# Query panels of a retrieval layer as three products of rounded operands, with the remainders taken by GpSimd

## What is computed

```
q = (xb @ w_q).reshape(PEER_BLOCK, PEER_HEADS, PEER_QDIM)       # 8 heads, 256 wide
s1 = jnp.einsum('phd,nd->phn', q[..., :half], subkeys[0])       # 128 keys
s2 = jnp.einsum('phd,nd->phn', q[..., half:], subkeys[1])
v1, i1 = lax.top_k(s1, PEER_TOPK)                               # 16 best of each half
v2, i2 = lax.top_k(s2, PEER_TOPK)
cand = (v1[..., :, None] + v2[..., None, :])                    # 256 candidates a head
cs, ci = lax.top_k(cand, PEER_TOPK)
...
g = jax.nn.softmax(cs); a = gelu(xb . u[e])                     # e: 16 of 16384 experts a head
y = sum over the chosen experts of g * a * v[e]
```

## Time and profile before

| what | value |
|---|---|
| three executions | 2624.45, 2632.71, 2630.9 us, median 2630.9 us |
| profiled execution, its own time | 2625.58 us |
| its span, first to last instruction | 2623.8 us |
| mean granted PE clock | 0.981 of full speed |
| busy: PE, PEld, DVE, ACT, POOL | 97%, 86%, 67%, 46%, 0% |
| query stage of layer 0 (first matmul to end of panel 7) | 735.67 to 798.21 us |
| query stage of layer 1 | 1753.61 to 1817.51 us |

### The profile page before, as it was taken

How to read it: one execution, slowest core, us unless ns; L and a number is a source line. 1 busy time by engine, 2 the same in 40 slices (tenths; PEclk the granted TensorE clock), 3 DMA queues, 4 the chain that set the end, 5 groups by cost and what they waited for, 6 DMA issues and landing times.

```text
span 2623.8 us, 42459 instructions
## 1 busy us (share of the span) xinstructions
PE 2543.8 (97%) x15716; PEld 2265.7 (86%) x15716; DVE 1765.4 (67%) x3521; ACT 1213.9 (46%) x2399; POOL 3.5 (0%) x10
## 2 busy tenths in 40 slices
PE   8999999999999999999999998989999999999997
PEld 4587889988889999999888887679999999888886
DVE  3662668865359977786788874537986787555554
ACT  2321124442214567775444443332457776455554
POOL 0000000000000000000000000000000000000000
PEclk9999999999999999999999999799999999999998
DMA  6562567656334544434777763123554443555553
GB/s 261 192 241 81 199 231 276 241 195 247 106 113 148 183 170 145 145 132 166 268 277 271 281 218 141 62 81 113 177 192 147 145 145 133 189 192 193 193 192 111
DMA packets 65348, 471.65 MB, mean 180 GB/s; under 512 B 7296, under 2 KB 7552, under 8 KB 8240
## 3 DMA queue, kind: packets, MB, share of 16 engines
q1 hardware_dynamic: 64656, 467.85, 50.1%
q10 hardware_dynamic: 272, 1.05, 0.1%
q0 software_dynamic: 272, 0.69, 0.1%
HBM read 468.51 MB, written 1.05 MB: 179 GB/s over the span
## 4 chain that ended last, share of the span: by engine, by line
PE 93%; DVE 5%; ACT 1%; issue 1%; DMA 1%; SPq 0%; DVEq 0%; ACTq 0%
PE bank L641 27%; PE bank L682 27%; PE bank L503 10%; PE bank L839 5%; PE bank L653 4%; PE bank L748 4%; PE bank L870 2%; PE bank L513 2%; PE bank L976 2%; PE bank L487 1%; PE bank L449 1%; PE bank L933 1%; DVE macc L1566 1%; PE bank L519 1%; PE bank L746 1%
## 5 line engine op out<-in xcount | busy, mean ns | idle before, releaser
L641 PE MATMUL bank<-h_split,t_split 128*128 128x256 f32 x6144 | 771.5, 285 | 4.8 <-DVE t_split L1796 3.7
L641 PEld LDWEIGHTS bank<-h_split,t_split 128*128 128x128 f32 x6144 | 745.4, 191 | 6.5 <-DVE t_split L1796 4.5
L1796 DVE TENSOR_TENSOR t_split<-ring,t_split 128x1024 fp32r<-128x1024 f32 x512 | 624.5, 1221 | 159.0 <-ACT t_split L1130 157.5
L682 PE MATMUL bank<-t_split,w_split 128*128 128x512 f32 x3072 | 703.9, 390 | 0.0
L682 PEld LDWEIGHTS bank<-t_split,w_split 128*128 128x128 f32 x3072 | 574.8, 188 | 118.8
L1135 ACT ACTIVATE t_split<-ring 128x1024 fp32r<-128x1024 f32 x256 | 271.6, 1061 | 357.9 <-PE bank L682 295.1
L1130 ACT ACTIVATE t_split<-ring 128x1024 fp32r<-128x1024 f32 x256 | 271.1, 1059 | 298.6 <-PE bank L641 273.1
L1828 DVE TENSOR_TENSOR w_split<-arena,w_split 128x256 fp32r<-128x256 f32 x256 | 108.8, 425 | 223.6 <-ACT w_split L1137 223.6
L503 PE MATMUL bank<-arena,ring 128*128 128x256 f32 x1024 | 231.4, 386 | 12.2 <-ACT arena L1090 7.9
L1071 ACT ACTIVATE arena<-bank 128x256 f32<-128x256 f32 (+2 forms) x160 | 64.3, 405 | 381.0 <-PE bank L503 154.0
L503 PEld LDWEIGHTS bank<-arena,ring 128*128 128x128 f32 x1024 | 195.8, 193 | 40.9 <-issue 9.4
(11 more groups left out here) (295 smaller groups left out, 2562.9 us busy)
## 6 DMA issues: line engine op xcount, KB each, us to landing
ring<-in_peer_u SPq DMA_DIRECT2D x128, 1024.0 KB, 4.9
ring<-in_peer_v SPq DMA_DIRECT2D x128, 1024.0 KB, 4.9
ring<-in_w_mod SPq DMA_DIRECT2D x24, 1024.0 KB, 5.1
ring<-in_mod_w SPq DMA_DIRECT2D x24, 1024.0 KB, 4.9
arena<-in_mod_w SPq DMA_DIRECT2D x24, 1024.0 KB, 6.5
ring<-in_w_in SPq DMA_DIRECT2D x22, 1024.0 KB, 4.9
ring<-in_w_up SPq DMA_DIRECT2D x22, 1024.0 KB, 5.0
ring<-in_peer_wq SPq DMA_DIRECT2D x16, 1024.0 KB, 4.9
```

What stands on the lines that cost most here:

```text
L641: last = mm(bank[:, 0:T], u[:, a_, k, :], h_split[:, b_, k, :], start=(k == 0 and a_ + b_ == 0), stop=(k == KT - 1 and a_ == 1))
L682: last = mm(BK[2 * tt + hf][:, :], w_split[:, j, a_, tt * P:(tt + 1) * P], t_split[:, 1 - j, b_, hf * 512:(hf + 1) * 512], start=(first an ...
L1796: TT(t_split[:, 1 - j, 1, :].rearrange("p (k c) -> p k c", k=KT), ring[:, r, :].rearrange(view, k=KT, j=2)[:, j], t_split[:, 1 - j, 0, :]. ...
```

## The change

- The 8 query panels of each layer are computed from split operands: high weights times high activations, low weights times high activations, high weights times low activations, 48 fp32r matmuls a panel. `query(h)` takes the place of `proj_cols`. For the first panel the products with the low activations come last.
- `q_split` holds two panels (double buffer, h % 2), each in a high and a low part. It lies at the start of the arena, over tiles of the mixer.
- ACT rounds the panels (`hi_q`, two halves a panel). The first two panels are rounded ahead of the squares of the norm, panel h+2 right after query tile 2h+1 is copied.
- POOL takes the remainders (`lo_q`, two subtractions of 128x1024 a panel), in its own queue between its transfers.
- A ring slot with a query panel is free when POOL is done with it, instead of when PE is.
- ACT writes the high activation tiles into `h_split` directly as it adds the shift; DVE forms the 8 low tiles with `scalar_tensor_tensor`. The whole-tile copy and subtraction (L1117, L1697) go.
- The picks and the candidate steps stay. A helper `squares(g)` of the gates is renamed.

```diff
@@ -249,7 +249,7 @@
 
         def peer_sections(l):
-            queries = [(a["peer_wq"][l], 8, "proj", 2)]
+            queries = [(a["peer_wq"][l], PH, "q_lo", 1)]
             return queries + [((a["peer_u"][l], a["peer_v"][l]), 2 * PAIRS, None, 0)]
@@ -283,10 +283,16 @@
                 DOWN += range(n, n + panels)
             n += panels if signal is not None else 0
 
+        QUERY, n = [], 0
+        for _, panels, signal, _ in SECTIONS:
+            if signal == "q_lo":
+                QUERY.append(range(n, n + panels))
+            n += panels if signal is not None else 0
+
         LOADS_BEFORE, PROJ_BEFORE, loads, n = [], [], [0, 0], 0
         projs = 0
         for _, panels, signal, per in SECTIONS:
-            projs += panels * (2 if signal == "up_lo" else per * (signal == "proj")) + 2 * PAIRS * (signal is None)
+            projs += panels * (2 if signal in ("up_lo", "q_lo") else per * (signal == "proj")) + 2 * PAIRS * (signal is None)
             if signal is None:
                 LOADS_BEFORE.append(list(loads))
                 PROJ_BEFORE.append(projs - 2 * PAIRS)
@@ -296,7 +302,8 @@
                     loads[r] += 16 * sum(m % RING == r for m in range(n, n + panels))
                 n += panels
 
-        H_PEER = (5, 8)
+        H_PEER = (4, 7)
+        q_split = nc.alloc_sbuf_tensor_at("q_split", [P, 2, 2, SLOT], f32r, offset=arena_at)
 
         BLOCKS = 2 * PAIRS
         RANKS = 2 * (PH + 1)
@@ -335,7 +342,7 @@
             sync.dma_start(ctxT[:, :, :], a["ctxT"]).then_inc(sems["ctx_in"], 16)
             sync.dma_start(xT[:, :, :], a["xT"]).then_inc(sems["x_in"], 16)
             n, freed, layer = 0, [], 0
-            total = {"proj": 0, "mod_acc": 0, "rows": 0, "up_lo": 0}
+            total = {"proj": 0, "mod_acc": 0, "rows": 0, "up_lo": 0, "q_lo": 0}
             at = {}
 
             def load(src):
@@ -355,7 +362,7 @@
                     at[id(dram)] = k0 + panels
                     for k in range(panels):
                         total[signal] += per
-                        if signal == "up_lo":
+                        if signal in ("up_lo", "q_lo"):
                             total["proj"] += 2
                         freed.append((signal, total[signal]))
                         load(dram[k0 + k])
@@ -653,11 +660,45 @@
                         last = mm(BK[6 + b][:, j * P:(j + 1) * P], P2[b][:, j, :], P1[b][:, j, :], start=True, stop=True)
                     last.then_inc(sems["g_mm"], 1)
 
+                def query(h):
+
+                    w = q_split[:, h % 2, :, :].rearrange("p s (k c) -> p s k c", k=KT)
+                    banks = []
+
+                    def part(j, a_, b_, first, last_one):
+
+                        if first:
+                            banks.append(ring_bank())
+                        for k in range(KT):
+                            if h == j == a_ == 0:
+                                fresh(k, 1, "h_lo" if b_ else "h")
+                            last = mm(banks[j][:, 0:T], w[:, a_, k, j * P:(j + 1) * P], h_split[:, b_, k, :],
+                                      start=(first and k == 0), stop=(last_one and k == KT - 1))
+                        if last_one:
+                            last.then_inc(sems["proj"], 1)
+
+                    pe.wait_ge(sems["q_hi"], 2 * (PH * l + h + 1))
+                    if h == 0:
+                        pe.wait_ge(sems["q_lo"], PH * l + 1)
+                        for j in range(2):
+                            part(j, 0, 0, True, False)
+                            part(j, 1, 0, False, False)
+                        for j in range(2):
+                            part(j, 0, 1, False, True)
+                    else:
+                        for j in range(2):
+                            part(j, 0, 0, True, False)
+                            part(j, 0, 1, False, False)
+                            if j == 0:
+                                pe.wait_ge(sems["q_lo"], PH * l + h + 1)
+                            part(j, 1, 0, False, True)
+                    e.skip(f"loaded{panel[0] % RING}", 16)
+                    panel[0] += 1
+
                 for h in range(PH):
-                    proj_cols(1, lambda k: hP[:, k, :], T, first=(h == 0))
+                    query(h)
                     if h:
                         keys(h - 1, 3)
-                pe.wait_ge(sems["h_split"], l + 1)
                 for b in range(BLOCKS):
                     for tt in range(2):
                         if b == STEP_AT[tt, "gates", 0] + 2:
@@ -1112,9 +1153,23 @@
                 A(root_buf, root_buf, ACT.Sqrt).then_inc(sems["ostd"], 1)
 
             def peer(l, scale_col, shift):
-                norm(xT, hP, shift, "proj")
-                act.wait_ge(sems["h"], H_PEER[l] * KT)
-                A(h_split[:, 0, :, :], hP, ACT.Copy).then_inc(sems["h_hi"], 1)
+                def hi_q(h):
+
+                    m = QUERY[l][h]
+                    act.wait_ge(sems[f"loaded{m % RING}"], 16 * (m // RING + 1 + (PAIRS * l if m % RING < 2 else 0)))
+                    for j in range(2):
+                        half = slice(j * D, (j + 1) * D)
+                        A(q_split[:, h % 2, 0, half], slot(m)[:, half], ACT.Copy).then_inc(sems["q_hi"], 1)
+
+                if l == 0:
+                    act.wait_ge(sems["o_done"], 1 + 8)
+                hi_q(0)
+                hi_q(1)
+                squares(xT, hP, "proj")
+                std_root()
+                for k in range(KT):
+                    act.wait_ge(sems["hs"], e.more("hs"))
+                    A(h_split[:, 0, k, :], hP[:, k, :], ACT.Identity, bias=modc[:, shift + k:shift + k + 1]).then_inc(sems["h"], 1)
                 qT = M5["qT"].rearrange("p (s t) -> p s t", s=16)
                 for r in range(2):
                     e.seen[f"loaded{r}"] = LOADS_BEFORE[l][r]
@@ -1140,8 +1195,12 @@
                     if s == 14:
                         if l == 0:
                             act.wait_ge(sems["mod_acc"], 56)
+                        act.wait_ge(sems["q_lo"], PH * l + 6)
                         hi_u(0)
                     evac("proj", qT[:, s, :], ACT.Copy)
+                    if s % 2 and s // 2 + 2 < PH:
+                        hi_q(s // 2 + 2)
+                act.wait_ge(sems["q_lo"], PH * (l + 1))
 
                 def gelu(b):
@@ -1693,8 +1752,10 @@
             def peer(l):
                 make_gain(0, 32, V("norm_g_2")[:, (2 * l + 1) * 8:(2 * l + 2) * 8])
                 norm(xT, hP, gain[:, 0, :], True)
-                dve.wait_ge(sems["h_hi"], e.more("h_hi"))
-                TT(h_split[:, 1, :, :], hP, h_split[:, 0, :, :].bitcast(f32), SUB).then_inc(sems["h_split"], 1)
+                for k in range(KT):
+                    dve.wait_ge(sems["h"], H_PEER[l] * KT + k + 1)
+                    STT(h_split[:, 1, k, :], hP[:, k, :], modc[:, 24 + k:25 + k], h_split[:, 0, k, :].bitcast(f32), ADD, SUB
+                        ).then_inc(sems["h_lo"], 1)
                 topv = M5["topv"].rearrange("p (t h s k) -> p t h s k", t=2, h=8, s=2)
                 topi = M5["topi"].bitcast(u32).rearrange("p (t h s k) -> p t h s k", t=2, h=8, s=2)
                 topif = M5["topif"].rearrange("p (h s k) -> p h s k", h=8, s=2)
@@ -2330,11 +2391,25 @@
             pool.dma_start(wgl, a["gla_gl"]).then_inc(sems["wgl_in"], 16)
             pool.dma_start(M3["wg2"][0:16, :], a["gla_wg2"]).then_inc(sems["wg2_in"], 16)
 
+
+            def lo_q(l, h):
+
+                for j in range(2):
+                    half = slice(j * D, (j + 1) * D)
+                    pool.wait_ge(sems["q_hi"], 2 * (PH * l + h) + j + 1)
+                    ins = pool.tensor_tensor(q_split[:, h % 2, 1, half], slot(QUERY[l][h])[:, half],
+                                             q_split[:, h % 2, 0, half].bitcast(f32), SUB)
+                ins.then_inc(sems["q_lo"], 1)
+
+            for h in range(PH):
+                lo_q(0, h)
             pool.wait_ge(sems["ranked"], 2 * PH)
             pool.dma_start(subT, a["subT"][1]).then_inc(sems["sub_in"], 16)
             pool.wait_ge(sems["modulated"], 2)
             pool.dma_start(M4["pos"].bitcast(i32), a["pos"]).then_inc(sems["pos_in"], 16)
             pool.dma_start(M4["band"], a["band"]).then_inc(sems["pos_in"], 16)
+            for h in range(PH):
+                lo_q(1, h)
 
 # ---- launch: the inputs laid out, nothing computed on them
```

More of the change, by code:

```diff
@@ L179, in build @@
                   "mod_acc", "mod_turn", "mod_bank", "proj", "turn", "bank4", "bank5", "sq", "ms", "var", "std", "h",
-                  "h_hi", "h_split", "hi", "split", "lb", "gate", "gates_f", "logf", "expo", "exps", "lin_in",
+                  "q_hi", "q_lo", "hi", "split", "lb", "gate", "gates_f", "logf", "expo", "exps", "lin_in",
                   "scores", "masked", "dstate", "state", "o_sum", "o_bank0", "o_bank1", "osq", "oms", "ovar", "ostd",
@@ L1163, in stored, with offsets @@
                       ).then_inc(sems["g_store"], 1)
```

(4 more changed lines are left out.)

## The result

The changed kernel takes 2613.72 us (median of four executions, 2613.18 to 2614.78), the kernel before 2630.89 (four executions, 2624.45 to 2632.71): 17.2 us less, ratio 0.9935 with a 95% interval of 0.9923 to 0.9946. Forecast were 18.4 us less and a time of 2612.

What follows compares the result with a forecast made beforehand. PE, busy 97% of the span, was taken to bound the kernel. Gains of 17.6 and 1.2 us less 0.4 make 18.4: 2607.2 from the profile's own time, 2612.5 from the median; predicted 2612, range 2603 to 2622.

Steps and rivals of the forecast that it cites:

- Steady panels: Query panels 1 to 7, both layers: 48 fp32r matmuls take 5.655 us instead of 6.91, saving 17.6 us.
- First panels: Panel 0 of each layer takes 8.90 us, as in the up projection; 1.2 us gained over both layers.
- Hand-over to DVE: End of the query stage: a DVE remainder between picks makes DVE 0.2 us late, lost in each layer.
- Sum: Whole kernel: 17.6 + 1.2 - 0.4 = 18.4 us saved.
- ACT, SP, slots: Early rounding of panels on ACT, and earlier slot release and panel transfers, cost or gain nothing.
- POOL: Remainder subtractions in the query stage take 2.4 us each, 4.8 in a period of 6.55, so hidden.
- Rival A: POOL's subtractions set the query panels' pace beyond 3.28 us each; at 4.7 us, 15.5 us slower, 2646; 7%.
- D: Query stage partly bound: subtractions of 3.3 to 4.4 us or delays of 1 to 2 a period; gain under 7.9; 8%.
- Rival B: POOL's reads hold up DVE's picks in the query stage; 20 us slower, 2651; 4%.
- Rival C: Only two-input DVE steps meet POOL, at the first `peer_u` remainder: 2.4 us lost a layer, 2617 us; 8%.
- likeliest case: The forecast by itself, whole kernel, with the first panels' bounds and the measured spread: 2603 to 2619 us.

Runs made afterwards that it cites:

- e7: Changed kernel plus nine float32 matmuls of constants after the norm's sum of squares, filling PE's wait before the first query panel; 2610.35 us.
- e8: Changed kernel with nine constant matmuls filling PE's wait behind the norm and the first panel's matmuls reordered to follow tile arrival; 2607.23 us.
- e1: Changed kernel with all query-panel remainders taken by DVE instead of POOL; 2627.37 us, ratio 0.9992 to the kernel before.
- e2: Changed kernel with POOL taking each remainder twice, with a wait on itself between; 2649.66 us, ratio 1.0072 to the kernel before.
- e3: Changed kernel plus 80 unused 128x512 POOL subtractions over the start of layer 0's hidden blocks, beside DVE's two-input steps; 2659.92 us.
- e9: The kernel before, unchanged, profiled once more; its profiled execution took 2632.31 us.

## Why the prediction was right

The time, its sign and its size are right; the terms, each by its own step:

- **Steady panels** (forecast 17.6 us): 6.91 - 5.605 = 1.305 us each, 14 of them 18.3 us. The up projection was a good price. Shown by both profiles' chains.
- **First panels** (+1.2): 15.41 - 5.60 = 9.81 against 8.83, and 15.54 - 5.60 = 9.94 against 10.18: 0.7 us lost instead of 1.2 gained. This is the term that was mis-sized, by 1.9 us, inside its bounds (+3.0 and -2.4). I took the 8.90 us of one panel of the up projection; the step that failed was to read one stretch as the price, where the length at the lower clock differs. In the changed kernel the granted clock was still 0.62 at 740 to 742 us, 6 to 8 us after the first matmul; in the up projection it was already 0.65 at 376 to 378, 4 to 6 us after it:

```profile
376.00:378.00 2.00, 2.00 (x14) 2.00 (x14) 1.93 (x6) 0.00 (x0) 0.00 (x0) 0.65 0.00 0
```

e7 shows that the clock is the cause: with it up, the first two panels take 13.36 us (734.78 to 748.14), the first so 7.76. What is left of the first panel then hangs on the order of the tiles (5.74 in e8).

- **Hand-over to DVE** (-0.4): 21.02 - 20.84 = 0.18 in each layer, as worked out.
- **Sum**: 18.3 - 0.7 - 0.4 = 17.2, the 17.2 of the two layers and of the medians.
- **ACT, SP, slots** (nothing): the halves of panel 1 ended near 720, the squares behind them before 722, and the step from the last projection's start to the first query matmul stayed 35.05 us (734.28 - 699.23; before 735.67 - 700.62).
- **POOL** (hidden, 2.4 us taken): 2.39 us each, hidden with 1.72 us a period to spare. The factor of two was an assumption without a row, and that it held to 0.01 us is luck; by the period of 6.49 us about 3.2 would have been hidden as well. The GPSIMD Engine Reference of the Trainium skill (section 3.1) leads to an estimate of 2.25 us; the measured 2.39 decides. Its advice to keep two-input work on VectorE (section 4.1) would have cost the whole gain here, as e1 shows.
- **Rival A** did not happen, and neither did **D** (no subtraction took over 2.42 us); e2 shows the mechanism of A and agrees with its formula at one point (18 against 19 us). **Rival B** is refuted: one search of a pick took 0.285 us beside POOL as before, and e3 shows 0.42 for the wider ones with POOL busy for 140 of 145 us. **Rival C** did not happen; e3 shows that it was only a matter of place. SBUF — State Buffer of the Trainium skill (Who interferes with whom) says that a VectorE instruction with two SBUF inputs contends with a GpSimd instruction that reads SBUF, and that one with at most one such input does not, outside the modes that use both ports, which casts and scalar steps can enter. e3 agrees on the two-input steps (1.22 to 1.92 us), the searches (0.42) and the cast (0.285 to 1.377); which mode the cast ran in, no run shows.
- **The arithmetic of the range and of B.** The terms of the likeliest case reach from 2604 to 2618, one us less at each end than the 2603 to 2619 stated. B's even point of 1.9 us of delay a period counts only what exceeds DVE's 0.9 us of waiting; with that it is 2.8.

Two errors partly cancel in the gain: the steady panels came out 0.7 us better and the first panels 1.9 worse. The forecast of 2612 also profited from being made against the median as well as the profile's own time: against the own time alone it would have been 2607, since that execution had 7 us less in the attention stage.

## What to carry to other kernels

Splitting an operand pays where PE is the bound and another engine has room for the remainder; count each engine's spare time in one period (here DVE 2.2 us before, POOL all), since the same work on DVE gives nothing back. GpSimd is good for such work while VectorE runs searches or reductions, not while it runs two-input steps, and casts and scalar steps may wait too: look at what VectorE does in the same microseconds. Behind every gap of PE, price the next matmuls by both levels of the clock, and try constant matmuls in the gap; and measure a stage from landmark to landmark, because an untouched stage can differ by more than the change is worth.

## What the runs showed of the hardware

- GpSimd held VectorE up also in steps with one SBUF input (e3): casts (0.285 to 1.377 us, L1812, twice; 0.227 to 1.205, L1832, once) and a scalar step (0.218 to 1.318, L1829, once); not in the searches (0.42) nor in a reduction of 2048 columns (2.28 and 2.27).
- The cost goes both ways: GpSimd's 128x512 subtraction took 1.80 us there instead of the 1.17 estimated without contention.
- Unchanged instructions between the two layers took 899.3 us in one profile and 906.0 to 906.5 in ten others (all but e3, whose extra work lies there), with a mean granted clock in the attention stage of 0.71 in the one (1665 to 1718 us), 0.52 in e9's profile of the same kernel (the same stretch) and 0.52 in the changed kernel's (1656 to 1716).
- Nine matmuls of constants (3.88 us in e7's chain) kept the granted clock at 2.4 GHz through the sparse matmuls that followed (1.00 from 734 to 740 us, where the changed kernel had 0.50 at 736 to 740).
